# Last attention's keys stored twice with zeroed halves, and the buffers of linear attention moved

## The chip, the cores and the metric

The kernel runs on one core of a Trainium2 chip, in float32. The metric is the device time of one execution, in microseconds (us); lower is better. Engines are named as in the profile: PE is TensorE (PEld its weight loads), DVE VectorE, ACT ScalarE, POOL GpSimd, SP SyncE.

## The reference

Three mixers run over 256 tokens of width 1024: a latent attention (16 heads), a block attention (16 heads), and then a second model's block, in which linear attention (4 heads) and a grouped attention stand side by side, followed by a mixture of 64 experts, two for each token. The change touches the grouped attention. It has 8 query heads and 2 key/value heads of width 64, is not causal, and sees all 256 keys:

```
q = rms_norm(aq) * q_gain;  k = rms_norm(ak) * k_gain      # per head, then rotated
s[h] = q[h] @ k[h // 4].T * 64 ** -0.5                       # 8 heads, 256 x 256
o[h] = softmax(s[h]) @ v[h // 4]
```

Its output is normed, laid beside the output of linear attention, and multiplied by w_out. The sum with the stream feeds the router and the experts.

## The kernel before

All stages are written out by hand, engine by engine; semaphores tie them together. Each engine, and each DMA queue, runs its own list in order. Tokens are two tiles of 128. Weight blocks of 2 MB come through a ring of slots on SP's queue, each load released when PE has finished with the block that held its slot (`proj_in_psum`). The blocks of w_in_2 are split by ACT and DVE into a rounded part and a rest, and multiplied three times (L1813).

One SBUF buffer, `qk` (8192 columns), is used again and again. Until the first blocks of w_in_2 are multiplied, its columns 0 to 1536 hold a rounded weight block (`values_hi`). After that it holds, for the last stage: `q_g` and `k_g`, the transposed queries and keys of the last attention, the linear attention's `exp_q`, `exp_k`, `exp_b`, `q_in`, `k_out`, `gla_t`, and `z_t` (L1427), the inputs of its decay. The two halves of `qk` then take expert 1's gate and up weights (`extra`).

Queries of two heads are transposed together (128 columns of `att_q`), so that in `q_g` an even head lies in rows 0 to 63 and the odd one in rows 64 to 127. Before the transposes DVE writes each key head twice, side by side, into `key2` (L1456); transposed, the same keys lie in rows 0 to 63 and again in rows 64 to 127 of `k_g`. DVE copies the transposes out of PSUM with `drain` (L1076): two of 512 columns for the queries, then two of 256 for the keys. Behind these on DVE stands the second half of the split of the last block of w_in_2 (L1120), then the states of linear attention (L1489, L1494).

All three attentions run through the same loop, `attention`, once on each engine. A unit is one head and one tile of queries; the last attention ("g") has 16. In step u PE multiplies the scores of unit u (L1842), transposes the probabilities of unit u - 3 (L1768) and multiplies them with the values of unit u - 4 (L1862). DVE takes the row maximum of unit u (L1252) and copies the transposes of unit u - 3 (L1076); ACT takes the exponential of unit u (L853). In the first two attentions each score is followed by a causal mask matmul (L1844), and their scores run over 128 rows: in the second attention by zeros in the other head's half of each query (`zero_other_heads` on POOL L691, `queries_out` on DVE L1389). In the last attention `scores_g` gives L1842 operands of 64 rows. At unit 2 it waits for ACT's copies of linear attention (`gla_copied`, L983), at unit 4 for DVE's sum (`gla_summed`, L1515). In units 4 to 7 ACT also squares two heads of linear attention each (L832); in unit 12 DVE also divides a tile's outputs (L1267, L1270). After the last unit PE transposes the mixed rows (L1768) and multiplies w_out (L1796).

POOL raises variances to the power -0.5 in the order of the table `RSQRT` (L699): among them "norm1t1", the stream's norm before w_in_2, then "qk", the head norms of the last attention, then "gla".

On SP's queue the first experts' loads follow: expert 1's up weights after `gla_summed`, its gate weights after the last score (`scores_in_psum`), and the others after further steps of PE. In the expert rounds each load waits until PE has used the slot (L2226, L2246), and PE waits for the load.

Of the kernel before, what the change touches and what calls it, by code (L numbers as in the profile page):

```python
# [26 lines left out]
P = 128  # L27
# [9 lines left out]
HD = 64  # L37
# [10 lines left out]
QH, KVH = 8, 2  # L48
# [43 lines left out]
JOB = {job: n for n, job in enumerate(JOBS)}  # L92
# [30 lines left out]
RSQRT = {}  # L123
# [64 lines left out]
def build(nc, t):  # L188

    where, const_cols = const_layout()  # L190
    with ExitStack() as ctx:
# [3 lines left out]
        def sem(name):  # L195
            return ctx.enter_context(nc.semaphore(name))
# [3 lines left out]
        tr_bank = bank[2:4]  # L200
# [46 lines left out]
        qk = sb("qk", [P, 8192])  # L247
# [29 lines left out]
        ln_row = tmp  # L277

        q_g = qk[:, 0:1024].rearrange("p (h s) -> p h s", h=QH // 2)
        k_g = qk[:, 1024:1536].rearrange("p (h s) -> p h s", h=KVH)  # L280
        exp_q = qk[:, 1536:2560].rearrange("p (d a s) -> p d a s", d=2, a=2)
        exp_k = qk[:, 2560:3584].rearrange("p (d a s) -> p d a s", d=2, a=2)
        exp_b = qk[:, 3584:4608].rearrange("p (d a s) -> p d a s", d=2, a=2)
        q_in = qk[:, 4608:5632].rearrange("p (d a s) -> p d a s", d=2, a=2)
        k_out = qk[:, 5632:6656].rearrange("p (t d n) -> p t d n", t=2, d=2)
        gla_t = qk[:, 6656:7680].rearrange("p (c s) -> p c s", c=4)
        z_t = qk[:, 7680:7936]
        gla_qk = stage[:, 0:2, :]
        decay = stage[:, 2:4, :]
        state = stage.rearrange("p n (a e) -> p n a e", a=2)  # L290
# [51 lines left out]
        proj_in_psum = sem("proj_in_psum")  # L342
        proj_in_sbuf = sem("proj_in_sbuf")
        tr_in_psum = sem("tr_in_psum")
        tr_in_sbuf = sem("tr_in_sbuf")
        masks_cast = sem("masks_cast")
        q_b_zeroed = sem("q_b_zeroed")
        power_set = sem("power_set")
        rsqrt_asked = sem("rsqrt_asked")
        rsqrt_done = sem("rsqrt_done")  # L350
# [312 lines left out]
        @block.gpsimd  # L663
        def _(pool):
            def scale_gla_heads(r, n):

                pool.wait_ge(rsqrt_done, n + 1)
                for tile in range(TILES):
                    o = wide[:, tile, 0:512]
                    o3 = o.rearrange("p (h d) -> p h d", h=4)  # L670
                    nc.gpsimd.tensor_tensor(o3, o3, r[:, 4 * tile:4 * tile + 4].rearrange(
                        "p (h a) -> p h a", a=1).to_broadcast([P, 4, GDV]), ALU.mult).then_inc(gla_normed, 1)
                    pool.wait_ge(gla_normed, tile + 1)
                    nc.gpsimd.tensor_tensor(o, o, gate[:, tile, 0:512], ALU.mult).then_inc(gla_gated, 1)

            def gate_outputs(kind):

                for n in range(4):
                    tile, group = n // TILES, n % TILES
                    half = slice(512 * group, 512 * group + 512)  # L680
                    pool.wait_ge(out_drained, OUT0[kind] + n + 1)
                    nc.gpsimd.tensor_tensor(wide[:, tile, half], wide[:, tile, half], gate[:, tile, half],
                                            ALU.mult).then_inc(mixed_ready, 1)

            def zero_other_heads():

                pool.wait_ge(proj_in_psum, JOB["moba_w_in", 0, 1] + 1)
                pairs = q_b.rearrange("p (c two) s -> p c two s", two=2)
                for odd in range(2):
                    rows = slice(HD * (1 - odd), HD * (2 - odd))  # L690
                    nc.gpsimd.memset(pairs[rows, :, odd, :], 0.0).then_inc(q_b_zeroed, 1)  # L691

            nc.gpsimd.memset(power[:], -0.5).then_inc(power_set, 1)
            pool.wait_ge(power_set, 1)
            for name, (n, a, w) in RSQRT.items():
                if name in ("ln0t0", "ln1t0"):
                    gate_outputs("a" if name == "ln0t0" else "b")
                pool.wait_ge(rsqrt_asked, n + 1)
                nc.gpsimd.tensor_tensor(rstd[:, a:a + w], var[:, a:a + w], power[:, 0:w], ALU.pow).then_inc(  # L699
                    rsqrt_done, 1)  # L700
                if name == "ln0t1":
                    zero_other_heads()
                if name == "gla":
                    scale_gla_heads(rstd[:, a:a + w], n)

# [340 lines left out]
        def _(dve):  # L1046
# [20 lines left out]
            tr = [0]  # L1067

            def drain(dst, gain=None, rows=P, width=512):

                n = tr[0]
                dve.wait_ge(tr_in_psum, n + 1)
                src = tr_bank[n % 2][0:rows, 0:width]
                src = src.rearrange("p (c s) -> p c s", s=P)
                if gain is None:
                    ins = nc.vector.tensor_copy(dst, src)  # L1076
                else:
                    blocks = width // P
                    ins = nc.vector.tensor_tensor(dst, src, gain.rearrange("p (c a) -> p c a", a=1).to_broadcast(  # L1079
                        [P, blocks, P]), ALU.mult)  # L1080
                ins.then_inc(tr_in_sbuf, 1)
                tr[0] += 1
# [48 lines left out]
            for half in range(2):  # L1131
                for tile in range(TILES):
                    n = TILES * half + tile
                    dve.wait_ge(x_hi_drained, n + 1)
                    at = (slice(None), slice(4 * half, 4 * half + 4), slice(tile * P, tile * P + P))
# [18 lines left out]
            for k in range(2):  # L1154
# [3 lines left out]
                for tile in range(TILES):  # L1158
                    at = slice(HD * tile, HD * tile + HD)
                    cos, sin = const("cos_g")[:, at], const("sin_g")[:, at].rearrange("p (d two) -> p d two", two=2)  # L1160
                    nc.vector.scalar_tensor_tensor(rope_g[:, 2 * k, at], cos, scale, g, ALU.mult, ALU.mult)
                    for x in range(2):
                        dst = rope_g[:, 2 * k + 1, at].rearrange("p (d two) -> p d two", two=2)[:, :, x]
                        last = nc.vector.scalar_tensor_tensor(dst, sin[:, :, x], scale, pairs[:, :, 1 - x],
                                                              ALU.mult, ALU.mult)
# [67 lines left out]
            for i in range(4):  # L1233
                last = nc.vector.tensor_copy(
                    stage[:, i, :].rearrange("p (h d) -> p h d", h=4)[:, :, NOPE:QKD],
                    key_rope[:, i % 2:i % 2 + 1, :].to_broadcast([P, 4, ROPE]))
# [211 lines left out]
            for tile in range(TILES):  # L1448
                at = slice(HD * tile, HD * tile + HD)
# [5 lines left out]
                for kv in range(KVH):  # L1455
                    last = nc.vector.tensor_copy(  # L1456
                        key2[:, tile, 128 * kv:128 * kv + 128].rearrange("p (c d) -> p c d", c=2),
                        att_kv[:, tile, HD * kv:HD * kv + HD].rearrange("p (c d) -> p c d", c=1).to_broadcast(
                            [P, 2, HD]))
# [6 lines left out]
            for n, (tile, way) in enumerate([(i, j) for i in range(TILES) for j in range(2)]):  # L1466
                at = slice(tile * P, tile * P + P)
# [8 lines left out]
            for tile in range(TILES):  # L1476
                drain(q_g[:, :, tile * P:tile * P + P])
            for tile in range(TILES):
                drain(k_g[:, :, tile * P:tile * P + P], width=2 * P)
            split_lo(block_of(("w_in_2", 4, 0)), (1,))  # L1480
            dve.wait_ge(gla_operands, 4)

# [275 lines left out]
        def _(pe):  # L1758
# [371 lines left out]
            def scores_g(h, tile, keys):  # L2130
                if tile == 0 and h == 2:
                    pe.wait_ge(gla_copied, 2)
                if tile == 0 and h == 4:
                    pe.wait_ge(gla_summed, 2)
                at = slice(HD * (h % 2), HD * (h % 2) + HD)
                return q_g[at, h // 2, tile * P:tile * P + P], k_g[at, h // (QH // KVH), 0:keys]

            def mixed_g_transposed(tile):
                pe.wait_ge(mixed_ready, 8 + tile + 1)
# [243 lines left out]
```

## Time and profile before

| what | value |
| --- | --- |
| median of 3 runs | 1407.85 us (1407.63 to 1408.08) |
| the profiled execution | 1395.12 us |
| its span in the profile | 1393.3 us |
| mean granted TensorE clock | 0.907 of full speed |
| PE, DVE, ACT, POOL busy | 1048.4, 479.4, 283.5, 36.1 us |
| HBM read | 462.07 MB, 332 GB/s over the span |

The profile shows one execution. A line of a group or of the timeline gives the start and the length in us, the engine, the line of the code, the operation, its output and its inputs, their partitions x elements, and how many instructions were merged; a bracket gives the idle time of the engine ahead of it and what ended that. A float32 matmul appears as two records, and a transpose as one.

### The profile page before, as it was taken

The numbers are of one execution on the slowest core, as the hardware profiler recorded it, in microseconds if no ns is written. First come the engines' busy times: TensorE is split into PE (matmuls) and PEld (weight loads), VectorE is DVE, ScalarE is ACT, GpSimd is POOL, SyncE is SP. The second block draws the span as 40 slices with busy tenths as digits, with TensorE's granted clock in tenths as the row PEclk, the third lists the DMA queues.
The fourth block names the chain that finished last, engine by engine and source line by source line (L and its number), as shares of the span: only waits on it lengthen the run. The fifth ranks groups of instructions, "written<-read, shape, count | busy, mean of one in ns | idle before, by whom it ended". The sixth has DMA issues, their size and how long they took to land.

```text
span 1393.3 us, 21666 instructions
## 1 busy us (share of the span) xinstructions
PE 1048.4 (75%) x9215; PEld 660.8 (47%) x9215; DVE 479.4 (34%) x1052; ACT 283.5 (20%) x610; POOL 36.1 (3%) x34
## 2 busy tenths in 40 slices
PE   8999999999999886675656766676665756757566
PEld 6857777878765542342323323233332423324232
DVE  4456785787954431221202212021120211212122
ACT  4334342544822111010001001010010110100000
POOL 0000101011102000000000000000000000000000
PEclk9999999999999998898889889798897988888898
DMA  8462255403575599999999999999999999999995
GB/s 308 136 242 70 70 203 181 155 31 131 183 313 236 211 377 426 425 428 425 427 426 425 428 426 425 428 426 425 428 427 425 428 425 427 427 425 427 427 424 239
DMA packets 69808, 463.75 MB, mean 333 GB/s; under 512 B 6722, under 2 KB 15108, under 8 KB 36356
## 3 DMA queue, kind: packets, MB, share of 16 engines
q1 hardware_dynamic: 68976, 460.48, 80.7%
q10 hardware_dynamic: 788, 2.66, 0.5%
q8 instruction: 31, 0.51, 0.1%
q14 instruction: 13, 0.11, 0.0%
HBM read 462.07 MB, written 1.05 MB: 332 GB/s over the span
## 4 chain that ended last, share of the span: by engine, by line
DMA 46%; PE 43%; DVE 6%; ACT 1%; issue 1%; SPq 1%; POOL 0%; DVEq 0%; ACTq 0%
DMA ring<-in_w_up 46%; PE bank L2226 14%; PE bank L1813 13%; PE bank L1796 5%; PE bank L1768 3%; PE bank L1842 2%; PE bank L1862 2%; PE bank L2246 1%; PE bank L1883 1%; SPq L552 1%; DVE ring_lo L1115 1%; PE bank L2300 1%; DVE ring_lo L1120 1%; PE bank L2208 1%; DMA res<-in_x 0%
## 5 line engine op out<-in xcount | busy, mean ns | idle before, releaser
L2226 PE MATMUL bank<-ring,expert_area 128*32 128x256 f32 x3968 | 323.3, 492 | 219.3 <-DMA ring<-in_w_up 219.0
L2226 PEld LDWEIGHTS bank<-ring,expert_area 128*32 128x32 f32 x3968 | 149.5, 137 | 385.8 <-DMA ring<-in_w_up 239.7
L1813 PE MATMUL bank<-ring_lo,xt_hi 128*128 128x512 f32 (+3 forms) x576 | 182.8, 386 | 0.6 <-DVE small L1305 0.4
L1650 DVE TENSOR_TENSOR expert_area<-expert_area,bank 128x128 f32<-128x128 f32 x64 | 18.3, 285 | 469.6 <-ACT expert_area L1008 469.6
L1008 ACT ACTIVATE expert_area<-bank 128x128 f32<-128x128 f32 x64 | 17.8, 278 | 618.0 <-PE bank L2226 618.0
L2246 PE MATMUL bank<-ring,consts 128*32 128x256 f32 x2016 | 121.8, 382 | 27.9 <-DVE consts L1652 27.9
L1813 PEld LDWEIGHTS bank<-ring_lo,xt_hi 128*128 128x128 f32 x576 | 104.1, 188 | 20.6 <-issue 3.7
L2246 PEld LDWEIGHTS bank<-ring,consts 128*32 128x32 f32 x2016 | 62.2, 109 | 69.2 <-DVE consts L1652 20.1
L1813 PE MATMUL bank<-ring_lo,xt_lo 128*128 128x512 f32 (+2 forms) x240 | 91.2, 380 | 0.0
L1796 PE MATMUL bank<-ring,xt 128*128 128x384 f32 (+1 forms) x192 | 75.7, 541 | 1.4 <-DVE xt L1079 0.8
L1656 DVE COPY consts<-bank 32x256 f32<-32x256 f32 x63 | 26.5, 421 | 132.7 <-PE bank L2246 132.7
L2300 PE MATMUL bank<-consts,expert_area 128*128 128x512 f32 x120 | 55.1, 601 | 16.2 <-DVE consts L1657 16.2
L1012 ACT COPY consts<-bank 32x256 f32<-32x256 f32 x63 | 22.8, 361 | 203.9 <-PE bank L2246 203.9
L2208 PEld LDWEIGHTS bank<-consts,wide 128*128 128x128 f32 x480 | 56.0, 192 | 7.2 <-issue 7.2
L2208 PE MATMUL bank<-consts,wide 128*128 128x128 f32 x480 | 56.0, 275 | 0.0
L2238 PE MATMUL bank<-consts,expert_area 128*128 128x128 f32 x64 | 21.0, 329 | 46.0 <-DVE expert_area L1650 46.0
L1115 DVE TENSOR_TENSOR ring_lo<-ring,ring_lo 128x2048 fp32r<-128x2048 f32 (+2 forms) x23 | 47.5, 2082 | 22.2 <-ACT ring_lo L762 22.0
L1674 DVE TENSOR_TENSOR res<-res,bank 128x512 f32<-128x512 f32 x60 | 41.3, 688 | 26.9 <-PE bank L2300 26.9
L1796 PEld LDWEIGHTS bank<-ring,xt 128*128 128x128 f32 x192 | 35.0, 190 | 30.5 <-issue 16.7
L1813 PEld LDWEIGHTS bank<-ring_lo,xt_lo 128*128 128x128 f32 x240 | 45.1, 188 | 8.5
L699 POOL TENSOR_TENSOR rstd<-var,power 128x1 f32<-128x1 f32 (+3 forms) x15 | 17.4, 1161 | 1107.2 <-DVE var L1744 920.1
L1842 PE MATMUL bank<-qk 128*128 128x256 f32 (+2 forms) x160 | 44.0, 369 | 1.6 <-DVE qk L1076 0.8
(286 smaller groups left out, 1149.1 us busy)
## 6 DMA issues: line engine op xcount, KB each, us to landing
ring<-in_w_down SPq DMA_DIRECT2D x62, 2048.0 KB, 24.8
ring<-in_w_gate SPq DMA_DIRECT2D x61, 2048.0 KB, 18.3
ring<-in_w_up SPq DMA_DIRECT2D x60, 2048.0 KB, 22.8
ring<-in_moba_w_kv SPq DMA_DIRECT2D x4, 2048.0 KB, 8.0
ring<-in_moba_w_in SPq DMA_DIRECT2D x4, 2048.0 KB, 8.6
ring<-in_w_in SPq DMA_DIRECT2D x3, 2048.0 KB, 7.8
ring<-in_mla_w_uq SPq DMA_DIRECT2D x4, 1152.0 KB, 5.6
ring<-in_mla_w_o SPq DMA_DIRECT2D x2, 2048.0 KB, 7.9
```

Of the source, the lines that this page charges most:

```text
L1115: last = nc.vector.tensor_tensor(lo[:, at], w[:, at], hi[:, at].bitcast(F32), ALU.subtract)
L1656: nc.vector.tensor_copy(expert_out[SLOTS * i:SLOTS * i + SLOTS, 512:768], bank[4][64:96, 0:256])
L1674: nc.vector.tensor_tensor(dst, dst, bank[5 + k % 3][:], ALU.add).then_inc(sum_added, 1)
L1768: last = nc.tensor.transpose(tr_bank[n % 2][0:cols, P * i:P * i + rows], x, ident[0:rows, 0:rows])
L1796: last = nc.tensor.matmul(proj_bank[n % 2][:, 0:width], xt[:, first + c, tile * P:tile * P + P], w[:, c, :], start=(c == 0), stop=(c == kc ...
L1813: last = nc.tensor.matmul(dst, x[at], w[:, c, :], start=(piece == 0 and c == 0 and w is hi and x is xt_hi), stop=(piece == 1 and c == 3 an ...
L1842: last = nc.tensor.matmul(dst[:, 0:keys], lhs, rhs, start=True, stop=not causal)
L1862: last = nc.tensor.matmul(out_bank[m // 8 % 2][:, HD * (h % 8):HD * (h % 8) + HD], probs_t[:, m % 2, P * k:P * k + P], values(h, k), start ...
L2208: last = nc.tensor.matmul(bank[c // 4][:, P * (c % 4):P * (c % 4) + P], routed[:, tile, c, :], onehot[:, tile, :], start=(tile == 0), stop ...
L2226: last = nc.tensor.matmul(bank[2][SLOTS * j:SLOTS * j + SLOTS, 0:256], picked[:, c, SLOTS * i:SLOTS * i + SLOTS], both[:, :, c, j // 2, j ...
L2246: last = nc.tensor.matmul(bank[4][SLOTS * j:SLOTS * j + SLOTS, 0:256], hidden_t[:, SLOTS * k:SLOTS * k + SLOTS], w[:, k, 256 * j:256 * j + ...
L2300: nc.tensor.matmul(bank[5 + k % 3][:], back[:, P * tile:P * tile + P], expert_out[:, 512 * half:512 * half + 512], start=True, stop=True). ...
```

## The change

`k_g` grows from 512 to 1024 columns: a copy for even heads, whose rows 64 to 127 are zero, and one for odd heads, whose rows 0 to 63 are zero. POOL fills the zero halves after "norm1t1" and after the projection that last read the weight block there; DVE drains each key transpose with two copies of 64 rows in place of one of 128; PE waits for the zeros before the first score and multiplies all 128 rows of `q_g`, which hold two heads, with the copy that is zero for the other head. The other buffers in `qk` move up by 512 columns, and `z_t` goes to the place of `q_g`.

```diff
--- before.py
+++ after.py
@@ -277,14 +277,14 @@
         ln_row = tmp
 
         q_g = qk[:, 0:1024].rearrange("p (h s) -> p h s", h=QH // 2)
-        k_g = qk[:, 1024:1536].rearrange("p (h s) -> p h s", h=KVH)
-        exp_q = qk[:, 1536:2560].rearrange("p (d a s) -> p d a s", d=2, a=2)
-        exp_k = qk[:, 2560:3584].rearrange("p (d a s) -> p d a s", d=2, a=2)
-        exp_b = qk[:, 3584:4608].rearrange("p (d a s) -> p d a s", d=2, a=2)
-        q_in = qk[:, 4608:5632].rearrange("p (d a s) -> p d a s", d=2, a=2)
-        k_out = qk[:, 5632:6656].rearrange("p (t d n) -> p t d n", t=2, d=2)
-        gla_t = qk[:, 6656:7680].rearrange("p (c s) -> p c s", c=4)
-        z_t = qk[:, 7680:7936]
+        k_g = qk[:, 1024:2048].rearrange("p (odd h s) -> p odd h s", odd=2, h=KVH)
+        exp_q = qk[:, 2048:3072].rearrange("p (d a s) -> p d a s", d=2, a=2)
+        exp_k = qk[:, 3072:4096].rearrange("p (d a s) -> p d a s", d=2, a=2)
+        exp_b = qk[:, 4096:5120].rearrange("p (d a s) -> p d a s", d=2, a=2)
+        q_in = qk[:, 5120:6144].rearrange("p (d a s) -> p d a s", d=2, a=2)
+        k_out = qk[:, 6144:7168].rearrange("p (t d n) -> p t d n", t=2, d=2)
+        gla_t = qk[:, 7168:8192].rearrange("p (c s) -> p c s", c=4)
+        z_t = qk[:, 0:256]
         gla_qk = stage[:, 0:2, :]
         decay = stage[:, 2:4, :]
         state = stage.rearrange("p n (a e) -> p n a e", a=2)
@@ -345,6 +345,7 @@
         tr_in_sbuf = sem("tr_in_sbuf")
         masks_cast = sem("masks_cast")
         q_b_zeroed = sem("q_b_zeroed")
+        k_g_zeroed = sem("k_g_zeroed")
         power_set = sem("power_set")
         rsqrt_asked = sem("rsqrt_asked")
         rsqrt_done = sem("rsqrt_done")
@@ -690,6 +691,15 @@
                     rows = slice(HD * (1 - odd), HD * (2 - odd))
                     nc.gpsimd.memset(pairs[rows, :, odd, :], 0.0).then_inc(q_b_zeroed, 1)
 
+            def zero_other_keys():
+
+                pool.wait_ge(rsqrt_done, RSQRT["norm1t1"][0] + 1)
+                pool.wait_ge(proj_in_psum, JOB["w_in_2", 1, 1] + 1)
+                for odd in range(2):
+                    rows = slice(HD * (1 - odd), HD * (2 - odd))
+                    nc.gpsimd.memset(k_g[rows, odd, :, :], 0.0).then_inc(k_g_zeroed, 1)
+                pool.wait_ge(k_g_zeroed, 2)
+
             nc.gpsimd.memset(power[:], -0.5).then_inc(power_set, 1)
             pool.wait_ge(power_set, 1)
             for name, (n, a, w) in RSQRT.items():
@@ -700,6 +710,8 @@
                     rsqrt_done, 1)
                 if name == "ln0t1":
                     zero_other_heads()
+                if name == "norm1t1":
+                    zero_other_keys()
                 if name == "gla":
                     scale_gla_heads(rstd[:, a:a + w], n)
 
@@ -1476,7 +1488,13 @@
             for tile in range(TILES):
                 drain(q_g[:, :, tile * P:tile * P + P])
             for tile in range(TILES):
-                drain(k_g[:, :, tile * P:tile * P + P], width=2 * P)
+                dve.wait_ge(tr_in_psum, tr[0] + 1)
+                for odd in range(2):
+                    rows = slice(HD * odd, HD * odd + HD)
+                    last = nc.vector.tensor_copy(k_g[rows, odd, :, tile * P:tile * P + P],
+                                                 tr_bank[tr[0] % 2][rows, 0:2 * P].rearrange("p (c s) -> p c s", s=P))
+                last.then_inc(tr_in_sbuf, 1)
+                tr[0] += 1
             split_lo(block_of(("w_in_2", 4, 0)), (1,))
             dve.wait_ge(gla_operands, 4)
 
@@ -2132,8 +2150,9 @@
                     pe.wait_ge(gla_copied, 2)
                 if tile == 0 and h == 4:
                     pe.wait_ge(gla_summed, 2)
-                at = slice(HD * (h % 2), HD * (h % 2) + HD)
-                return q_g[at, h // 2, tile * P:tile * P + P], k_g[at, h // (QH // KVH), 0:keys]
+                if tile == 0 and h == 0:
+                    pe.wait_ge(k_g_zeroed, 2)
+                return q_g[:, h // 2, tile * P:tile * P + P], k_g[:, h % 2, h // (QH // KVH), 0:keys]
 
             def mixed_g_transposed(tile):
                 pe.wait_ge(mixed_ready, 8 + tile + 1)
```

## Rows read from the trace of the kernel before

**Rows 1.** The page: the span, and TensorE's busy time, share and instructions.

```profile
span 1393.3 us, 21666 instructions
PE 1048.4 (75%) x9215; PEld 660.8 (47%) x9215; DVE 479.4 (34%) x1052; ACT 283.5 (20%) x610; POOL 36.1 (3%) x34
```

**Rows 2.** The chain that ended last, in order of time: start us, us, what; after the last attention, then the experts.

```profile
430.06 0.67 PE bank L1768 x4
...
525.14 20.77 DMA ring<-in_w_up
```

**Rows 3.** Timeline of the last attention, PE and PEld: start us, length us, engine, line, operation.

```profile
411.44 0.70 PE L1842 MATMUL bank<-qk 64*128 64x256 f32 x2
...
412.82 0.70 PE L1842 MATMUL bank<-qk 64*128 64x256 f32 x2
...
413.45 0.20 PEld L1768 LDWEIGHTS bank<-consts,probs 128*128 128x128 f32 x2 [0.33 <-ACT probs L853]
413.45 0.44 PE L1768 MATMUL bank<-consts,probs 128*128 128x128 f32 x2
...
413.72 0.56 PE L1862 MATMUL bank<-att_kv,probs_t 128*128 128x64 f32 x4
...
426.69 0.70 PE L1842 MATMUL bank<-qk 64*128 64x256 f32 x2
```

**Rows 4.** Timeline of the first attention, second tile (256 keys), PE.

```profile
143.69 0.65 PE L1842 MATMUL bank<-qk 128*128 128x256 f32 x2
144.17 0.22 PE L1844 MATMUL bank<-causal_b,ident_b 128*128 128x128 bf16 x1
144.23 0.39 PE L1768 MATMUL bank<-consts,probs 128*128 128x128 f32 x2
144.45 0.56 PE L1862 MATMUL bank<-val,probs_t 128*128 128x64 f32 x4
144.85 0.65 PE L1842 MATMUL bank<-qk 128*128 128x256 f32 x2
```

**Rows 5.** One stretch: length, busy PE, PEld, DVE, ACT, POOL, granted clock, DMA share, GB/s.

```profile
411.44:426.69 15.25, 15.25 (x90) 10.87 (x89) 9.75 (x26) 9.61 (x44) 6.24 (x5) 1.00 0.96 405
```

**Rows 6.** Timeline: the first four scores of the last attention, and their maxima on DVE.

```profile
408.48 1.45 PE L1842 MATMUL bank<-qk 64*128 64x256 f32 x8
...
409.99 1.42 DVE L1252 TENSOR_REDUCE small<-bank 128x1 f32<-128x256 f32 x4
```

**Rows 7.** Timeline of the last attention: ACT in unit 6, DVE in unit 12.

```profile
415.40 0.47 ACT L853 ACTIVATE probs<-bank,small 128x256 f32<-128x256 f32 x1 [0.24 <-DVE small L1252]
...
422.81 0.69 DVE L1270 TENSOR_TENSOR wide<-bank,small 128x512 f32<-128x512 f32 x1
```

**Rows 8.** Timeline: DVE's last key copy and what follows it, and PE's use of the split.

```profile
383.97 0.43 DVE L1076 COPY qk<-bank 128x256 f32<-128x256 f32 x1 [0.18 <-PE bank L1768]
...
384.31 2.73 DVE L1120 SCALAR_TENSOR_TENSOR ring_lo<-ring,gain_cols,ring_lo 128x512 fp32r<-128x512 f32 x4
...
389.00 0.73 PE L1813 MATMUL bank<-ring_lo,xt_hi 128*128 128x512 f32 x2
...
389.09 0.87 DVE L1494 SCALAR_TENSOR_TENSOR stage<-stage,qk,bank 128x256 f32<-128x256 f32 x2 [0.85 <-PE bank L2069]
```

**Rows 9.** POOL: its fills as a group (busy us, mean ns; idle before), and the power "qk".

```profile
L691 POOL MEMSET qk<- 64x2048 f32 x2 | 3.6, 1806 | 56.2 <-PE bank L1813 56.1
...
355.83 3.97 POOL L699 TENSOR_TENSOR rstd<-var,power 128x20 f32<-128x20 f32 x1 [14.06 <-DVE var L1439]
```

**Rows 10.** Groups on DVE between 200 and 260 us, by form: busy us, mean ns; idle before.

```profile
L1389 DVE COPY qk<-bank 64x512 f32<-64x512 f32 x8 | 5.5, 689 | 3.6 <-PE bank L1768 3.5
...
L1076 DVE COPY qk<-bank 128x512 f32<-128x512 f32 x4 | 2.6, 686 | 2.5 <-PE bank L1768 2.5
```

**Rows 11.** SP's queue in order of time: the load of expert 1's gate weights.

```profile
427.41 0.34 SPq L552 DMA_DIRECT2D qk<-in_w_gate  x1
```

**Rows 12.** One stretch ahead of the expert rounds; columns as in rows 5.

```profile
472.00:478.00 6.00, 5.69 (x50) 5.01 (x53) 4.40 (x17) 1.72 (x4) 0.00 (x0) 0.72 0.01 3
```

## The prediction

> **What bounds the kernel now.** I read the page first: the span is 1393.3 us and TensorE is busy 75% of it [rows 1]. The chain that ended last names two regimes. From 525 us on it is the expert weights' transfers, one after another [rows 2]; before that it is work on the core. So the question is whether the change moves the moment at which the expert rounds begin. The last attention ends in the transposes of the mixed rows, and these stand on that chain at 430.06 [rows 2]; its scores are what the change touches.
>
> Next, the instructions of that attention in order of time [rows 3]. Each score is a pair of records at L1842 over 64 rows; then come the transposes of an earlier head's probabilities (L1768) and an earlier head's output (L1862), both over 128 rows. From the fifth score (411.44) to the sixteenth (426.69) are 11 equal periods: 15.25 / 11 = 1.386 us. TensorE is busy in all 15.25 us, VectorE in 9.75 and ScalarE in 9.61, at a granted clock of 1.00 (the 2.4 GHz level) [rows 5]. So TensorE sets this period, though the row of the transposes' weight load says that it waited 0.33 us for ScalarE's exponential [rows 3]. That label is only the last semaphore of the wait: the head transposed there is three units old.
>
> Then the same loop in the first attention, where scores run over 128 rows and keys are also 256 wide [rows 4]. Its period is 144.85 - 143.69 = 1.16 us, with one instruction more (the causal mask, L1844).
>
> **The change, part by part.** The period by its starts:
>
> Score to transposes: 413.45 - 412.82 = 0.63 over 64 rows [rows 3]; 144.17 - 143.69 = 0.48 to the mask over 128 [rows 4]. Saved 0.15. Transposes to output: 413.72 - 413.45 = 0.27 against 144.45 - 144.23 = 0.22, saved 0.05. Output to next score: 1.386 - 0.63 - 0.27 = 0.49 against 144.85 - 144.45 = 0.40, saved 0.09. The mask's own slot, 144.23 - 144.17 = 0.06, does not exist here. New period: 1.16 - 0.06 = 1.10 us; saved 0.28 us per unit. The rows say that a change between 64 and 128 rows costs some 0.14 us each way, and that the arithmetic over the added zero rows costs nothing.
>
> How many: 11 periods, plus the way into the fifth score and out of the sixteenth, together about one more, hence 12 x 0.28 = 3.4 us. The units after 426.69 have no scores and merely start earlier.
>
> Scores 0 to 3 stand apart: they follow each other without transposes between them, 8 records in 1.45 us [rows 6], and become longer, not shorter. The second rival has their price. I take 0: VectorE reads the first only at 409.99, after linear attention's sum, and reduces all four in 1.42 us.
>
> Can the other engines keep 1.10? In units 4 to 7 ScalarE also squares two heads; even there it idled 0.24 us of a period [rows 7], so it needs 1.386 - 0.24 = 1.15. It falls behind 0.05 a unit for four units, against exponentials that are made three units ahead. VectorE's one long extra is L1270 of 0.69 us at 422.81 [rows 7], in a unit where the reduction and the copy take 0.36 each by the rate of [rows 6] (1.42 / 4): 0.72 + 0.69 + 0.2 = 1.6 us. That is 0.5 over the period; the output waits for a copy made one unit before, so most is absorbed. I subtract 0.1, bounds 0 and 0.5.
>
> **VectorE's key copies** become four of 64 x 256 instead of two of 128 x 256. Copies of 64 and 128 partitions cost the same in the second attention (689 and 686 ns at 512 columns) [rows 10]. A 256-column copy takes 0.43 and the next starts 0.34 later [rows 8], so 2 x 0.34 = 0.68 more. They come after the query copies, which end the chain of VectorE there. Behind them is the split of the last weight block, 384.31 + 2.73 = 387.04, moving to 387.7; TensorE starts on it at 389.00 [rows 8]. Then the first states; VectorE sat idle 0.85 us before 389.09 [rows 8]. So 0, and 0.68 if that cover were gone.
>
> **GpSimd** gets two fills of 64 x 512. The fills of 64 x 2048 took 1806 ns each [rows 9]; a quarter is 0.45, so about 0.9 with both, bounds 0.9 and 3.6. They wait for the second block's projection. What stands behind them on that queue is the head norms' power at 355.83, before which GpSimd sat idle 14.06 us [rows 9]; it is asked for only after the same projection has been drained and VectorE has squared and summed every head. TensorE needs the zeros at 408.48 [rows 6]. So 0; without that cover at most the 0.9. The added waits on GpSimd and TensorE are long met by then, and no DMA is added. **The moved buffers** keep sizes and strides, no load gets a new condition, and the moved ones alias only data already read: 0.
>
> **After the attention.** Expert 1's gate weights are issued when the last score is done, at 427.41 [rows 11]; this moves 3.3 us earlier with it, and so do the later loads, each released by TensorE (the transfers in flight then may let it land a little later than that, but it is not used before the expert rounds). The loads ahead of it keep their places on the queue. I therefore carry the whole gain into the expert rounds, where transfers follow each other without a gap and the end moves with their start. A granted clock of 0.72 in 472 to 478 [rows 12] means (1 - 0.72) x 6 = 1.7 us of clock lost; an earlier arrival could change this either way by as much.
>
> **Sum.** -3.4 + 0.1 = -3.3 us, bounds -2.9 to -3.9 before the clock. The profiled execution took 1395.12 us, span plus 1.8 outside it; the median of the runs is 1407.85, 0.9% more, and the same step taken from it gives 1404.5.
>
> **Rivals.**
> *The wait was real.* If the 0.33 us were ScalarE's after all, scores over 128 rows would save nothing in the loop and the time would stay 1407.9. For it speaks the label alone; against it the equal periods with TensorE busy throughout, and the 1.16 of [rows 4]. Chance 0.09. That the kernel does not do what it says would look the same and is in this chance.
>
> *The lost pairing.* A head's scores use the upper or the lower 64 rows, alternately. A lone score takes 0.70 us [rows 3], but four of them 1.45 [rows 6]: two neighbours take hardly more than one, so they run side by side. Over 128 rows they must queue, and one holds TensorE for 0.48 [rows 4]: two of the four are no longer free, at most 2 x 0.48 = 0.96 us more for scores 0 to 3. If that is not hidden behind VectorE, the gain is 3.3 - 1.0 = 2.3 us and the time 1405.5. Chance 0.09. Beside this: "TensorE: Matmul & The Clock Gate", Part 3, of the Trainium skill says that matmuls on different row groups of the array run concurrently. By that rule alone a full-height score would be worth avoiding everywhere; the trace agrees for neighbours, but in the steady loop no two scores are neighbours.
>
> *Another engine takes the period.* If the copy that feeds the output came late in every unit, the period would stop near ScalarE's 1.15 to 1.25 instead of 1.10: 12 x (0.05 to 0.15) = 0.6 to 1.8 us given back, time 1405.1 to 1406.3. Against it speak VectorE's 0.72 of work a unit. Chance 0.11.
>
> *Slower: the clock.* VectorE and ScalarE hold TensorE idle before the fifth score. If the granted clock fell to the 1.2 GHz level there and stayed through the loop, a stretch of 12 x 1.10 = 13 us would double and 13 - 3.3 = 10 us be lost, 1417.6; it decides from 3.3 us of lost clock, that is 6.6 us at the low level. The clock was 1.00 here with longer gaps [rows 5], and the new scores fill some of that gap. Chance 0.05.
>
> A stretch at the low clock near 475 that disappears would bring 1.7 us more (1402.8), 0.02. The forecast has the other 0.64.
>
> **Numbers.** 0.2%, about what a measurement of this kernel can tell from no change, is 2.8 us. Faster by more: 0.64 + 0.02 = 0.66. Within: 0.09 + 0.09 + 0.11 = 0.29. Slower by more: 0.05. The range from 1403.1 to 1407.1 holds the forecast with its bounds, the pairing and the engine rivals, and half of the clock's 1.7 on either side (-3.9 - 0.85, and 1406.3 + 0.8); it leaves out no change, the clock's loss and its gain, 0.16.
>
> **What would show it.** The scores' records read 128x256 and start 1.10 us apart over 11 periods, the weight load of the transposes has lost its 0.33 us of idle, and L1768 of the mixed rows starts near 426.7, with expert 1's gate issued near 424.1. If the period stays 1.386, the account of the row change is wrong. If it is 1.10 but the last wait for in_w_up ends as late as before, the gain was lost in the hand-over to the experts. If the first four scores hold back VectorE's first reductions, it is the pairing.

## The result and the profile after

The kernel after takes 1390.23 us (median of 4 runs, 1389.62 to 1391.21). The kernel before, run beside it on the same chip, takes 1407.96 (1407.63 to 1408.75). The ratio is 0.9874, 95% interval 0.9857 to 0.9891: 17.7 us less, where 3.3 were predicted, and outside the predicted range.

The page of the kernel after: the span, the engines, the granted clock in 40 slices.

```profile
span 1388.1 us, 21672 instructions
PE 1044.4 (75%) x9215; PEld 660.1 (48%) x9215; DVE 479.5 (35%) x1054; ACT 283.1 (20%) x610; POOL 37.0 (3%) x36
PEclk9999999999999999898888888788997888988888
```

Against [rows 1] the span is 5.2 us shorter, not 17.7. The difference is between the executions. The one profiled execution of the kernel before took 1395.12 us, 12.7 less than the median of its runs; the profiled one of the kernel after took 1389.98, 0.25 below its median. The sections below are about this gap. First, what the two profiles show.

Timeline of the last attention after, PE: start us, length us, engine, line (18 higher than before), operation.

```profile
407.09 1.97 PE L1860 MATMUL bank<-qk 128*128 128x256 f32 x8
...
417.82 0.65 PE L1860 MATMUL bank<-qk 128*128 128x256 f32 x2
418.30 0.38 PE L1786 MATMUL bank<-consts,probs 128*128 128x128 f32 x2
418.52 0.56 PE L1880 MATMUL bank<-att_kv,probs_t 128*128 128x64 f32 x4
418.92 0.65 PE L1860 MATMUL bank<-qk 128*128 128x256 f32 x2
...
425.70 1.09 PE L1786 MATMUL bank<-consts,wide 128*128 128x128 f32 x8 [0.29 <-DVE wide L1550]
```

One period is 418.92 - 417.82 = 1.10 us, against 1.386 [rows 3]: the score holds TensorE for 0.48 instead of 0.63, the transposes for 0.22 instead of 0.27, the output for 0.40 instead of 0.49. The fifth score starts at 410.05 and the sixteenth at 422.40, so the mean over 11 periods is 1.123. From the first score to the transposes of the mixed rows it is 425.70 - 407.09 = 18.61 us, against 430.06 - 408.48 = 21.58 [rows 2, 6]: 2.97 less.

The loop of the kernel after in one stretch (length; busy PE, PEld, DVE, ACT, POOL; granted clock; DMA share; GB/s):

```profile
410.05:422.48 12.43, 12.43 (x91) 11.06 (x90) 9.25 (x27) 9.20 (x45) 5.03 (x5) 1.00 1.02 431
```

TensorE is busy throughout at a clock of 1.00, as in [rows 5]. The gain then travels to the experts: the gate weights of expert 1 are issued 4.3 us earlier than in [rows 11], and the transfer that stands on the chain at 525.14 in [rows 2] starts 4.5 us earlier. SP's queue, and the chain that ended last, after:

```profile
423.09 0.34 SPq L553 DMA_DIRECT2D qk<-in_w_gate  x1
```

```profile
520.64 20.60 DMA ring<-in_w_up
```

Of the 5.2 us between the two profiles, 2.97 arise in the loop, 1.39 ahead of it (408.48 - 407.09) and about 0.8 behind it.

### The profile page after: what moved, and what is told of

Read it like the earlier page. It is cut to its first block, busy times and chain, and to the rows that moved or that the text cites. A ratio compares the mean times of both kernels' runs of the same rounds, so it can differ in the third digit from the quotient of the medians.

```text
span 1388.1 us, 21672 instructions
## 1 busy us (share of the span) xinstructions
PE 1044.4 (75%) x9215; PEld 660.1 (48%) x9215; DVE 479.5 (35%) x1054; ACT 283.1 (20%) x610; POOL 37.0 (3%) x36
## 4 chain that ended last, share of the span: by engine, by line
DMA 47%; PE 43%; DVE 6%; ACT 1%; issue 1%; SPq 1%; POOL 0%; DVEq 0%; ACTq 0%
DMA ring<-in_w_up 46%; PE bank L2245 14%; PE bank L1831 13%; PE bank L1814 5%; PE bank L1786 2%; PE bank L1860 2%; PE bank L1880 2%; PE bank L2265 1%; SPq L553 1%; PE bank L1901 1%; DVE ring_lo L1127 1%; PE bank L2319 1%; DVE ring_lo L1132 1%; PE bank L2227 1%; DVE qk L1088 0%
## 5 line engine op out<-in xcount | busy, mean ns | idle before, releaser
L1860 PE MATMUL bank<-qk 128*128 128x256 f32 (+1 forms) x160 | 43.9, 363 | 1.5 <-DVE qk L1088 0.8
```

What stands on the lines that cost most here:

```text
L1860: last = nc.tensor.matmul(dst[:, 0:keys], lhs, rhs, start=True, stop=not causal)
```

## The experiments

The theories were these. *A common step*: the difference between the profiled execution and the runs lies all over the program, and the rest of the gain has small causes. *The clock*: the granted clock falls to the lower of its two levels in the last attention of the kernel before, in most executions, and not in the kernel after. And two about the parts: that the moved buffers or the doubled keys bring something by themselves. In the expectations, theory A is the common step with the predicted gain beside it, and theory B lays all of the 17.7 us to the change; theory C says that the scores' rows in the loop decide the clock, theory D that the work ahead of the loop does, and theory E that the rows bear on the fall alone, not on the return. The runs of the kernel before that stood beside the experiments are counted under e1.

### e1: the kernel before again, unchanged

> The kernel before, unchanged, once more. Theory A (the change is worth its 0.28 us a unit, some 3.4 us, and the other 13 us of the measured 17.7 are a difference between executions or loadings of the same program): this copy falls near 1395 like the first profiled execution, or near 1408 like the timed runs, and can differ from the other copy of itself by up to 13 us. Theory B (the 17.7 us all come from the change): 1408 in every timed run, ratio 1.000 within 0.001, and a profile that shows where 13 us more than 1393.3 are spent.

Measured: median 1407.73 us in 10 executions, nine from 1406.92 to 1408.18 and one at 1395.15. The 68 timed executions of the kernel before that stood beside the first result and the experiments make the same two groups: 59 at 1406.1 to 1409.0 and 9 at 1394.4 to 1395.7. For the 64 that stood beside the experiments the mean granted clock of each execution is on record too, and it splits them in the same way: 0.893 to 0.900 in the 55 long ones, 0.906 to 0.909 in the 9 short ones. The profile that the prediction read came from the rare group. This time the profiled execution took 1406.92, so the usual one can be read. The page of e1, and stretches of it (columns as in [rows 5]):

```profile
span 1405.1 us, 21666 instructions
PE 1061.9 (76%) x9215; PEld 669.1 (48%) x9215; DVE 480.4 (34%) x1052; ACT 283.4 (20%) x610; POOL 36.1 (3%) x34
PEclk9999999999986999888978889888898888988888
```

```profile
411.00:412.00 1.00, 1.00 (x8) 0.67 (x7) 0.80 (x3) 1.00 (x7) 0.00 (x0) 1.00 1.01 434
412.00:413.00 1.00, 1.00 (x4) 0.58 (x3) 0.29 (x1) 1.00 (x7) 0.00 (x0) 0.58 0.97 418
...
420.00:430.00 10.00, 10.00 (x33) 6.93 (x33) 3.67 (x11) 2.26 (x8) 5.10 (x5) 0.50 0.56 238
430.00:436.00 6.00, 6.00 (x19) 3.81 (x20) 2.31 (x5) 1.74 (x6) 1.12 (x1) 0.50 0.00 0
...
442.00:444.00 2.00, 2.00 (x16) 1.73 (x16) 1.45 (x4) 0.00 (x0) 0.00 (x0) 0.78 1.03 442
```

The clock row of the page (PEclk, 40 slices of about 35 us) has an 8 and a 6 where the row of after has nines. Closer up, the clock is 1.00 until 412 and 0.50, the 1.2 GHz level, from then until about 443, though TensorE is recorded busy in every microsecond. The timeline of e1, PE, shows what it costs:

```profile
412.15 1.22 PE L1842 MATMUL bank<-qk 64*128 64x256 f32 x2
...
414.67 1.22 PE L1842 MATMUL bank<-qk 64*128 64x256 f32 x2
...
437.29 1.22 PE L1842 MATMUL bank<-qk 64*128 64x256 f32 x2
...
442.43 1.38 PE L1768 MATMUL bank<-consts,wide 128*128 128x128 f32 x8
```

A pair of records of one score takes 1.22 us instead of 0.70, and from the sixth score to the sixteenth 10 periods take 437.29 - 412.15 = 25.14 us, 2.51 each. That is 25.14 - 10 x 1.386 = 11.3 us more. From the sixteenth score to the mixed transposes it is 5.14 us, against 430.06 - 426.69 = 3.37 [rows 2, 3], 1.8 more. Together 13.1. From the first score (407.81) to the mixed transposes e1 needs 34.62 us, 13.04 more than the 21.58 of the rare execution. The medians of the two groups (1407.7 and 1394.9) are 12.8 apart: the clock in this stretch accounts for the gap, and the common step falls.

The Trainium skill, "TensorE: Matmul & The Clock Gate", Part 1, says of the low level: "the default state is throttled, and activity releases the throttle." By busy time the trace does not agree: TensorE's records leave no gap in these 31 us, and the clock stayed at the low level. The measurement decides here. What the records do not show is how much of the array is at work inside them.

### e2: the kernel after again, unchanged

> The changed kernel, once more, beside the kernel before on the same chip. Theory A: span 1388 to 1389, and a ratio of 0.996 to 0.998 if the kernel before runs at its lower level here, 0.987 if at its upper one. Theory B: ratio 0.987 whatever the chip.

Measured: 1390.34 us (1390.30 to 1391.30, 4 executions), ratio 0.9894 (0.9841 to 0.9946). With the first four, eight executions of the kernel after lie within 1.7 us of each other. None is 13 us longer.

### e3: all of the change but the rows of the scores

```diff
 # on the kernel after, in scores_g
-return q_g[:, h // 2, ...], k_g[:, h % 2, h // (QH // KVH), 0:keys]
+at = slice(HD * (h % 2), HD * (h % 2) + HD)
+return q_g[at, h // 2, ...], k_g[at, h % 2, h // (QH // KVH), 0:keys]
```

> The changed kernel with its scores multiplied over 64 rows again; the doubled keys, the fills, the extra copies and the moved buffers stay. Theory A (the gain of the loop is the change of row height at each score): the period goes back from 1.10 to 1.386 us, the mixed rows' transposes 3.4 us later, time 3.4 us over the changed kernel. Theory B, moved buffers give 13 us: time at most 4 us over the changed kernel and 13 under the kernel before. If the scores carry everything, it is at 1408.

Measured: 10 of 11 executions at 1406.79 to 1409.15 and one, the profiled one, at 1395.21; ratio 1.0007 (0.9987 to 1.0027). With the zeros filled and the keys kept twice, but 64 rows multiplied, both groups of the kernel before are back, at the same times. Its scores start at 411.32, 412.71, 414.10 and 415.49: a period of 1.39. So fills, extra copies and moved buffers bring nothing and cost nothing that can be seen, and all of the gain hangs on the rows of the scores.

### e4: only the moved buffers

```diff
 # on the kernel before: q_g and k_g as they were
-exp_q = qk[:, 1536:2560]...
+exp_q = qk[:, 2048:3072]...
...
-z_t = qk[:, 7680:7936]
+z_t = qk[:, 0:256]
```

> The kernel before with nothing but linear attention's buffers moved 512 columns up and z_t put at column 0. Theory A: the same time as the kernel before, within 1 us, period 1.386. Theory B, placement gives 13 us: 1395.

Measured: 8 of 10 at 1406.34 to 1408.83, two at 1394.27 and 1395.54; ratio 0.9986 (0.9954 to 1.0019). The moved buffers are worth nothing by themselves.

### e5: 128 rows in the first four scores alone

```diff
 # on the kernel after, in scores_g
+if tile == 0 and h < 4:
+    return q_g[:, h // 2, ...], k_g[:, h % 2, h // (QH // KVH), 0:keys]
+at = slice(HD * (h % 2), HD * (h % 2) + HD)
+return q_g[at, h // 2, ...], k_g[at, h % 2, h // (QH // KVH), 0:keys]
```

> The changed kernel, with only scores 0 to 3 over 128 rows and scores 4 to 15 over 64. Theory C (the loop of 64-row scores lets the granted clock fall to the 1.2 GHz level in most executions and holds it there until the loop ends, 13 us; over 128 rows it stays at 2.4 GHz): two levels again, near 1395 and 1408, most executions at the upper one, period 2.5 us there. Theory D (the clock is decided by the work just ahead of the loop, the first four scores and the wait behind them): one level, near 1395, and no execution near 1408.

Measured: four executions at 1392.80 to 1393.68 and one, the profiled one, at 1407.24; ratio 0.9898 (0.9881 to 0.9914). A stretch of the profiled one:

```profile
413.00:414.00 1.00, 1.00 (x7) 0.95 (x6) 0.83 (x2) 0.98 (x7) 0.00 (x0) 0.66 0.88 360
414.00:420.00 6.00, 6.00 (x20) 4.08 (x19) 1.70 (x4) 2.47 (x14) 0.00 (x0) 0.50 1.00 419
```

The loop is the old one, over 64 rows. Yet with four scores over 128 rows ahead of it the fall is rarer: one in five, against seven in eight of the kernel before in the same experiment and 59 in 68 in all. The fall is still possible, and once it is there it stays in the loop. The four undisturbed executions are also shorter than those of e3 and e4 (1394.27 to 1395.54), though their loop is no shorter; this comes back under *Open*.

### e6: 128 rows from the fifth score on

```diff
 # as e5, but with the condition turned round
+if tile == 1 or h >= 4:
+    return q_g[:, h // 2, ...], k_g[:, h % 2, h // (QH // KVH), 0:keys]
```

> The reverse: scores 0 to 3 over 64 rows, scores 4 to 15 over 128. Theory C: one level, 1390 to 1392, granted clock 1.00 through the loop, period 1.10. Theory D: two levels, about 1391 and some 10 us or more above.

Measured: 1389.97 to 1391.08 us in 4 executions, ratio 0.9877 (0.9860 to 0.9893), the time of the kernel after. The clock is 1.00 from 411 to 428. The first four scores of e6, over 64 rows:

```profile
407.84 1.45 PE L1860 MATMUL bank<-qk 64*128 64x256 f32 x8
```

This is 1.45 us, as in [rows 6]; over 128 rows they take 1.97. The lost pairing is real, 0.52 us, and hidden. By the rule of the Trainium skill that stands in the prediction ("TensorE: Matmul & The Clock Gate", Part 3), the version of e6 should have been the better one; the rule holds for these neighbours, by the same two numbers, and changes no time.

### e7: a transpose over 128 rows after each score of the kernel before

```diff
 # on the kernel before, after each score
+if kind == "g":
+    last = nc.tensor.transpose(dst[:, 256:256 + P], ident, ident)
```

> The kernel before with one transpose of the identity over 128 rows behind each 64-row score, written to unused columns of the score's bank. Theory C1 (the clock goes by how much of the array's rows the work keeps busy): the filler raises that, so fewer or no executions near 1408, and a loop about 12 x 0.06 = 0.7 us up to 1.5 us longer, 1396. Theory C2 (any 64-row matmul in the loop, or the change between heights, brings the clock down): two levels as before, 1396 and 1408 or more.

Its output is not used. The profile records the transpose as one matmul. Measured: 1396.57 to 1397.02 us in 4 executions, ratio 0.9923 (0.9907 to 0.9940). Timeline and stretches of e7:

```profile
415.13 0.70 PE L1842 MATMUL bank<-qk 64*128 64x256 f32 x2
415.76 0.33 PE L1847 MATMUL bank<-consts 128*128 128x128 f32 x1
...
416.63 0.70 PE L1842 MATMUL bank<-qk 64*128 64x256 f32 x2
```

```profile
409.00:411.00 2.00, 2.00 (x8) 1.00 (x7) 1.54 (x4) 0.72 (x4) 0.00 (x0) 1.00 1.00 426
415.00:425.00 10.00, 10.00 (x60) 7.21 (x60) 5.58 (x17) 5.11 (x22) 3.30 (x3) 1.00 1.01 429
```

Work was added, the period grew to 1.50 us, and the program is 11 us faster than before, since the clock no longer falls (mean clock 0.907 to 0.909 in all four). That confirms the clock as the cause of the large part. But the run does not say why it stays up: the added transposes also fill TensorE's wait ahead of the fifth score, where it is recorded busy for 2.00 of 2.00 us between 409 and 411, against 0.86 in e1.

### e8: the kernel after, with a longer gap ahead of the fifth score

```diff
 # on the kernel after: ACT, ahead of softmax_units("g")
+for _ in range(14):
+    link(nc.scalar.activation(small[:, 195:196], const("ones")[:, 0:1], ACT.Exp))
```

> The changed kernel with 14 small chained operations on ScalarE ahead of its first exponential, which hold TensorE idle some 4 us longer before the loop. Theory C: the clock falls in that gap, but comes back within the loop over 128 rows, so the time is the gap's 4 us plus at most 5 more, 1394 to 1400, and not the 13 of a whole loop at the low level. Theory D: once it is low ahead of the loop it stays low through it, 4 + 13 us, near 1407.

Measured: the profiled execution took 1394.12 us. A second one read 3381.37 us; there is no profile of it, its cause is unknown, and it did not come back in the ten executions of e12. Stretches of e8:

```profile
411.00:412.00 1.00, 0.28 (x2) 0.29 (x3) 0.00 (x0) 0.97 (x5) 0.00 (x0) 0.77 0.88 377
412.00:413.00 1.00, 1.00 (x4) 0.76 (x3) 0.42 (x1) 1.00 (x7) 0.00 (x0) 0.50 1.09 467
...
414.00:415.00 1.00, 1.00 (x5) 0.90 (x5) 0.14 (x1) 0.90 (x6) 0.00 (x0) 0.52 0.84 360
415.00:416.00 1.00, 1.00 (x9) 0.90 (x8) 0.72 (x2) 0.26 (x1) 0.00 (x0) 1.00 0.95 401
```

TensorE stood idle for 2.62 us, from 409.1 to 411.7, and here the clock of the kernel after did fall, at about 411.5. But it was back after less than 4 us, inside the loop.

### e9: the same gap, scores over 64 rows

```diff
 # on e8: the edit of e3
```

> The kernel of the third experiment (doubled keys, but scores over 64 rows) with the same 14 small operations ahead of the first exponential. Theory C, the loop's rows hold the clock: it falls in the gap as in the eighth experiment, and stays at 0.50 until after the last score, some 12 x 1.1 = 13 us lost, 1407 to 1412 in every execution. Theory E (the rows of the scores bear only on whether it falls, not on whether it comes back): it is back within 5 us, 1397 to 1403.

Measured: all 8 executions at 1409.46 to 1411.56, ratio 1.0040 (1.0011 to 1.0070). Stretches of e9:

```profile
413.00:414.00 1.00, 1.00 (x4) 0.33 (x3) 0.42 (x1) 1.00 (x6) 0.00 (x0) 0.76 0.97 418
414.00:415.00 1.00, 1.00 (x6) 0.93 (x6) 0.63 (x2) 1.00 (x7) 0.00 (x0) 0.50 1.03 426
...
430.00:440.00 10.00, 10.00 (x33) 6.93 (x33) 4.14 (x11) 2.82 (x11) 4.24 (x4) 0.50 0.00 0
446.00:450.00 4.00, 4.00 (x20) 3.20 (x19) 2.57 (x5) 0.63 (x2) 0.00 (x0) 0.79 0.92 315
```

e8 and e9 differ in the rows of the scores alone. With 128 rows the clock comes back in the loop; with 64 rows it comes back only after the last score, more than 30 us later.

### e10 and e11: a filler in the loop alone, over 128 or over 64 rows

```diff
 # on the kernel before, after each score from the fifth on; e10:
+if kind == "g" and u >= 4:
+    last = nc.tensor.matmul(dst[:, 256:256 + P], ident, ident, start=True, stop=True)
 # e11: ident[at, :], ident[at, :] with the score's 64 rows
```

> The kernel before with one float32 matmul of the identity with itself over 128 rows behind each of scores 4 to 15, and nothing behind scores 0 to 3, so that the work ahead of the loop is that of the kernel before. Theory C: clock 1.00 through the loop, one level, 1396 to 1398. Theory D (what stands ahead of the loop decides): two levels, most executions about 13 us above.

> The same, with the added matmul over the 64 rows of its own score. It adds as many records and columns as the one over 128 rows, and no change of row height. If the height of the work in the loop is what keeps the clock up: two levels, most executions near 1408 or above. If any added work keeps it up: one level, 1396 to 1398.

Measured: e10 has four executions at 1396.41 to 1397.98 and six at 1412.00 to 1414.55, ratio 1.0020 (0.9970 to 1.0070). e11 has all ten at 1411.42 to 1413.84, ratio 1.0043 (1.0023 to 1.0062). Stretches of e10's profiled execution, one of the six:

```profile
411.00:412.00 1.00, 1.00 (x7) 1.00 (x7) 0.60 (x2) 0.91 (x7) 0.00 (x0) 0.60 0.92 393
...
430.00:440.00 10.00, 10.00 (x36) 7.58 (x34) 3.87 (x10) 2.42 (x9) 3.94 (x4) 0.50 0.00 0
```

So 128-row fillers between 64-row scores are not enough, either to prevent the fall or to end it. Four undisturbed of ten cannot be told from the seven of 31 of the kernel before that stood beside them, so e10 does not show that such fillers help at all. e7 held the clock in 4 of 4, with four fillers more ahead of the loop, but its fillers were transposes (one record of 0.33 us) and those of e10 plain matmuls (two records, 0.50 us). That the ones ahead of the loop make the difference fits e5, and is not shown by this pair. The simple form of the theory, that some more work over all rows in the loop settles it, fell with e10. Fillers of 64 rows did not keep the clock up in any of ten.

### e12: e8 again, ten times

> The eighth experiment again, for more executions: 1393 to 1395 each, the clock low for some 4 us from about 411 and back within the loop.

Measured: 1393.36 to 1396.64 us in 10 executions, ratio 0.9935 (0.9905 to 0.9964). Stretches of e12:

```profile
413.00:418.00 5.00, 5.00 (x20) 4.22 (x19) 2.00 (x6) 3.24 (x18) 0.00 (x0) 0.50 0.98 416
418.00:422.00 4.00, 4.00 (x31) 3.70 (x29) 2.71 (x8) 2.27 (x10) 0.00 (x0) 0.94 1.04 438
```

The clock was low from 411.6 or so to 418.5, and back for the rest of the loop. The gap and the short low stretch together cost 3 to 6 us over the kernel after; no execution stayed low, which would have shown above 1400. No version was faster than the kernel after.

## Why the prediction was wrong

**The step that failed** stands at its end: "The profiled execution took 1395.12 us, span plus 1.8 outside it; the median of the runs is 1407.85, 0.9% more, and the same step taken from it gives 1404.5." The 12.7 us were passed over as a factor common to the whole program. They were one stretch of 31 us, in the very loop that the change touches, in which the clock stands at 1.2 GHz in the usual execution (59 of 68 by their times, and e1's profile) and stood at 2.4 GHz in the one that was profiled. With it fell the clock rival's ground, "The clock was 1.00 here" [rows 5]: true of that execution only. The rival had the mechanism, but put it into the kernel after. That its price agrees (13 us, measured 13.0) is partly luck: it doubled twelve periods of 1.10, where the trace has ten periods of 1.386 that grew by 1.13 each and 1.8 us more behind the last score. The fallen clock was the usual case of the kernel before, and the change takes it away. e3 shows that by undoing the rows alone, and e8 with e9 that the rows decide whether a fallen clock comes back.

**The sum.** 17.7 us = 13.0 from the clock, 3.0 from the loop, and 1.7 left over. Undisturbed executions against each other say nearly the same: eleven of the kernel before (the first profile's and e1's among them) have a median of 1394.9, eight of after one of 1390.3, so 4.6, where 3.3 was predicted; 12.8 for the clock and 4.6 make 17.4.

**The period.** Right: 1.10 us in most units, 1.123 in the mean, and 2.97 us from the first score to the mixed transposes, against 3.3 (bounds 2.9 to 3.9). The ways into and out of the loop, counted as a twelfth period, were worth less: from the first score to the fifth nothing (2.96 us both times), from the sixteenth to the mixed transposes 0.07. Its reason fits: the starts are now those of the first attention [rows 4], and the arithmetic over zeros costs nothing. That makes 0.28 us for two changes between 64 and 128 rows; the 0.14 each is this sum halved, for 0.05 of it lies between the transposes and the output, both over 128 rows. Beside it: the Trainium skill, "TensorEngine Tiling (Array Packing)", Key Properties, says that changing the tiling mode drains TensorE. The trace agrees in so far as a unit without the two changes is 0.28 us shorter.

**The stall by VectorE's long operation.** About right: 0.1 was subtracted. Unit 13 was longer by 0.20, 421.31 - 420.01 = 1.30 us, where the output waited for VectorE's copy. The weight load of the output there, and the group of the transposes' weight loads over the 11 periods, after:

```profile
420.81 0.52 PEld L1880 LDWEIGHTS bank<-att_kv,probs_t 128*128 128x128 f32 x4 [0.16 <-DVE probs_t L1088]
...
L1786 PEld LDWEIGHTS bank<-consts,probs 128*128 128x128 f32 x22 | 3.1, 141 | 1.1
```

The 0.33 us that the transposes' weight load showed for the exponential [rows 3] is gone: 0.1 us of idle a unit is left, and ScalarE is no longer named for it. The period fell to 1.10 us with ScalarE's work unchanged, so the wait was not what set it.

**The first four scores.** Right: longer by 0.52 (bound 0.96) and hidden. VectorE in the kernel after:

```profile
407.91 0.75 DVE L1533 TENSOR_TENSOR wide<-wide,bank 128x256 f32<-128x256 f32 x2 [2.76 <-ACT wide L995]
408.69 1.41 DVE L1264 TENSOR_REDUCE small<-bank 128x1 f32<-128x256 f32 x4
```

It reaches the first maximum at 408.69, straight from linear attention's sum. e6 puts the pairing back and gains nothing that can be seen.

**VectorE's copies and GpSimd's fills.** Both hidden, as predicted. After, on DVE, PE and POOL:

```profile
382.07 1.75 DVE L1494 COPY qk<-bank 64x256 f32<-64x256 f32 x4
383.85 2.74 DVE L1132 SCALAR_TENSOR_TENSOR ring_lo<-ring,gain_cols,ring_lo 128x512 fp32r<-128x512 f32 x4
...
387.70 0.73 PE L1831 MATMUL bank<-ring_lo,xt_hi 128*128 128x512 f32 x2
...
348.88 1.09 POOL L700 MEMSET qk<- 64x512 f32 x2 [8.45 <-PE bank L1831]
354.56 3.90 POOL L709 TENSOR_TENSOR rstd<-var,power 128x20 f32<-128x20 f32 x1 [4.58 <-DVE var L1451]
```

The split ends at 386.6 and TensorE uses it at 387.70. The two fills took 1.09 us (estimated 0.9), and GpSimd was idle for 4.58 us behind them. **The moved buffers**: nothing, by e4.

**After the attention.** Carried whole: a lead of 4.36 us at the mixed transposes (2.97 and the 1.39 of arrival) is 4.5 at the transfer on the chain [rows 2]. The mixed transposes stood at 425.70 and not near 426.7, since the attention began 1.39 us earlier, which the prediction did not have.

**The other rivals.** *The wait was real* and *another engine takes the period* fell with the period of 1.10, *the lost pairing* with e6.

**Open.** First, what it is in the 64-row scores that lets the clock fall: the half of the rows that stands empty, the changes between 64 and 128 rows, or the longer period, in which less is computed. Every experiment that changed the rows of the loop's scores changed all three, and no run separates them. Second, what decides in a single execution of the kernel before whether the clock falls; e5 shows only that the work ahead of the loop shifts how often. The profiles give a lead. Of those with 64-row scores in the loop and no added gap, five fell, and their first score starts at 407.28 to 407.99 (e1, e4, e5, e10, e11); three did not, and theirs starts at 408.37 to 408.48 (the first profile, e3, e7). Eight profiles of seven kernels do not prove a rule. Third, about 1.6 us between undisturbed executions: in the first pair of profiles 0.8 of it lies behind the loop and some ahead. But the first score starts anywhere from 407.1 to 408.5 in the profiles, and in e1, a kernel before, at 407.81, so the arrival cannot be laid to the change. If the undisturbed executions of the kernel before are those that arrive late, as the lead has it, the 4.6 us hold up to 1.4 of arrival that is not the change's; this is not shown.

## What to carry to other kernels

Hold the profiled execution's time against the median of the runs before reading a row of it: where they are 0.9% apart, the profile may show an execution in which the stretch of interest behaves otherwise than usual, and the gap is the first thing to explain, not a factor. The mean granted clock of each single execution (here 0.893 to 0.900 against 0.906 to 0.909) tells the groups apart. Look for the second group among single executions, and profile again until both are seen. In float32 matmuls whose operands fill half the rows, zeros in the other half cost nothing here, save 0.28 us for each unit in which they avoid two changes of mode, and kept TensorE at 2.4 GHz in a stretch where it otherwise mostly stood at 1.2.

## What the hardware showed that was not expected

- TensorE recorded busy without a break for 31 us and more, with scores over 64 rows among work over 128, at a granted clock of 0.50 (e1, e9). The same loop with scores over 128 rows ran at 1.00 and, when a gap had brought the clock down, was back at 1.00 after 3.4 us (e8) and 6.8 us (e12). In e1 and e9 it came back only once the last score was done.
- Added work made the program faster: 16 unused 128-row transposes, 11 us less (e7). Twelve unused matmuls over 128 rows, in the loop alone, left 6 of 10 executions at the low clock (e10), and twelve over 64 rows all of 10 (e11).
- At the low level the period went from 1.386 to 2.51 us, a factor of 1.81 and not of 2, while VectorE and ScalarE worked at their own pace beside it.
